# Sparse attention stage: unscaled weights turned, the three branches' values kept apart, scale factors formed later and applied to the results

## The chip, the cores and the metric

One core of a Trainium2 chip runs the whole program. The metric is the device time of one execution in microseconds (us). TensorE (PE in the rows) does matrix products and transposes, VectorE (DVE) and ScalarE (ACT) elementwise work, GpSimd (POOL) and SyncE (SP) issue the transfers (DMA) beside what else they do. The engines run on their own and meet only at semaphores.

## The reference, cut to what matters

The model is one hybrid decoder layer: a convolution branch, a gated DeltaNet branch, sparse attention, then cross attention and an MLP. The change touches sparse attention alone. Its part for the prompt, for each of 8 heads and each of 8 blocks of 128 queries, with three branches of keys (compressed, selected, window):

```python
def masked_softmax(s, mask):
    s = jnp.where(mask, s.astype(F32), -1e30)
    m = jnp.max(s, axis=-1, keepdims=True)
    e = jnp.exp(s - m) * mask
    return e / jnp.maximum(jnp.sum(e, axis=-1, keepdims=True), 1e-30)
...
o_c = jnp.einsum('bgrqn,bngd->bqgrd', p_c.astype(vc.dtype), vc)
o_s = jnp.einsum('bgrqk,bgqkd->bqgrd', p_s.astype(vs.dtype), vs)
...
gt = jax.nn.sigmoid(gl).reshape(Bh, Th, 3, NSA_KV, NSA_GQ, 1)
...
o = gt[:, :, 0] * o_c + gt[:, :, 1] * o_s + gt[:, :, 2] * o_w
```

So each branch's exponentials are divided by their row sum, multiplied by that branch's gate and by the values, and the three results are added. The division and the gate are one factor for each query, branch and head. The factor can be applied to the exponentials (before) or to the branch's result (after).

## The kernel before

The sparse stage is the function `sparse`. It works on a list of 50 items in a fixed order: 32 prompt items (4 head pairs of 8 query blocks `tt`; one item holds both key groups `g`) and 18 sets of the sample's cache pages (items of kind SET), which stand between the prompt items from the fifth on, two sets for three prompt items. A prompt item has `tt + 1` blocks of 128 selected keys, up to 5 window blocks, and 4(tt + 1) compressed keys. Everything is float32.

The same order of steps is written out by hand on three engines:

- TensorE, step i: `score(i, c)` writes the scores of item i in chunks of up to 512 columns into a ring of two bank pairs (chunk G waits until chunk G - 2 has been read: `pe.wait_ge(biased, G - 1)`). Between the chunks, `merged` puts the tail of item i - 3: `turn` transposes its weights in groups of two key blocks, `values` multiplies them with the values, two groups later. One bank region collects all three branches of an item.
- VectorE, step i: `biases(i)` adds the position bias to each chunk, takes the maxima, and ends with the negated maximum (`negm_ready`). Then `scales(i - 1)` waits until ScalarE has all exponentials of item i - 1, forms the six factors (three small instructions, L2071 to L2075), and multiplies the exponentials with them in six instructions (L2080), whereupon `probs_ready` lets TensorE turn them.
- ScalarE, step i: `exps(i - 1)` (six exponentials with their sums, L1911), interleaved with `copies(i - 3)`, the copies of the turned weights out of the PSUM banks (L1931), and `keep_result` (L1949), the copy of a finished item to the output.

The factor on the exponentials is this:

```python
last = V.tensor_scalar(src, src, scale[:, p, g, x:x + 1], None, ALU.mult)
```

SyncE's queue loads, in order of the item that frees the place, the pages of the sets (a ring of three sets of 2 MB, shared with GpSimd's queue) and, for each new head pair, queries and bias rows (`load(r)`: 5 transfers, 2.2 MB).

Of the kernel before, what the change touches and what calls it, by code (L numbers as in the profile page):

```python
# [13 lines left out]
ALU = mybir.AluOpType  # L14
# [8 lines left out]
P = 128  # L23
# [1521 lines left out]
def sparse(nc, t, u, kv, toeplitz, ident, by_token, out, gdn, spill, kvp, space, pages, kct, vc_past, past_space, early):  # L1545
# [15 lines left out]
    PAGES, NEWKEYS = "pages", "new"  # L1561
# [40 lines left out]
    first_chunk, first_group = [0], [0]  # L1602
    for i in range(NI):
        first_chunk.append(first_chunk[-1] + n_chunks(i))
        first_group.append(first_group[-1] + len(groups(i)))
    BEHIND = 2
# [7 lines left out]
    with ExitStack() as ctx:  # L1614
# [12 lines left out]
        assert next_place(nc) - ranking_at >= 3 * 16 * PAGE * 2 and early.end - early.at >= 16 * PAGE * 2  # L1627
# [5 lines left out]
        cnt, flag, addm, near = S("count", [P, IH]), S("flag", [P, NBLK]), S("block_mask", [P, 2, NBLK]), S("near", [P, 2, PAGE])  # L1633
        oc, acc = S("set_out", [P, 2, 2, P]), S("sample_sum", [P, 2, P])
# [4 lines left out]
        def alias(name, shape):  # L1639
# [5 lines left out]
        ring = alias("ring", [P, 2, HB, 4, 2 * PAGE])  # L1645
        third = nc.alloc_sbuf_tensor_at("nsa_ring_third", [P, HB - 1, 4, 2 * PAGE], F32, offset=ranking_at)
        third_last = nc.alloc_sbuf_tensor_at("nsa_ring_third_last", [P, 4, 2 * PAGE], F32, offset=early.at)
# [9 lines left out]
        region = lambda i: ps[:, O_BANK + i % REGIONS, 0:P]  # L1657
        sem = phase_semaphores(ctx, nc, "nsa_")
# [5 lines left out]
        (scores_mm, biased, cleared, max_ready, negm_ready, exp_ready, chain, probs_ready, pt_mm, pt_out, pv_mm, o_mm, o_out) = (  # L1664
            sem(s) for s in ("scores_mm", "biased", "cleared", "max_ready", "negm_ready", "exp_ready", "chain", "probs_ready",
                             "pt_mm", "pt_out", "pv_mm", "o_mm", "o_out"))
# [71 lines left out]
        def _(pe):  # L1738
# [3 lines left out]
            def score(i, c):  # L1742
                kind, n, tt = items[i]
                G = first_chunk[i] + c
# [42 lines left out]
            def values(i, k):  # L1787
# [16 lines left out]
                else:  # L1804
                    for j, (x, col, vb) in enumerate(group):
                        w = 4 * (tt + 1) if x == CMP else P
                        for g in range(2):
# [61 lines left out]
            for i in range(NI + LAG):  # L1869
# [11 lines left out]
                tailing = [(i - LAG, s) for s in range(0, len(groups(i - LAG)), 2)] if i >= LAG else []  # L1881
                for which, (n, k) in merged(scoring, tailing):
                    if which:
# [3 lines left out]
                        values_up_to(first_group[n] + pair[-1] + 1 - BEHIND)  # L1887
                    else:
# [8 lines left out]
        def _(act):  # L1897
# [43 lines left out]
            def keep_result(i):  # L1941
                kind, n, tt = items[i]
                act.wait_ge(o_mm, i + 1)
                if kind == SET:
                    x, hf, c = sets[n]
                    dst = oc_set[:, hf, c, :] if x == SLC else oc[:, hf, 0, :]
                else:
                    dst = out[:, n, tt * P:(tt + 1) * P]
                act.activation(dst, region(i), ACT.Copy).then_inc(o_out, 1)  # L1949
# [48 lines left out]
        def _(dve):  # L1998
# [13 lines left out]
            def set_biases(i):  # L2012
                x, hf, c = sets[items[i][1]]
                G, dst = first_chunk[i], s_[:, i % SLOTS, 0, :]
# [12 lines left out]
                add_biases(stat_of(items[i][1]), pieces, (biased, first_chunk[i + 1])).then_inc(negm_ready, 1)  # L2027

            def biases(i):
# [12 lines left out]
                for c, pieces in enumerate(chunks(tt)):  # L2042
                    G = first_chunk[i] + c
# [13 lines left out]
                dve.wait_ge(biased, first_chunk[i + 1])  # L2057
# [119 lines left out]
            for i in range(NI + 1):  # L2177
# [4 lines left out]
                if i >= 1:  # L2182
                    scales(i - 1)
# [1012 lines left out]
```

## Time and profile before

| | us |
|---|---|
| median of 3 runs (2793.57 to 2802.07) | 2799.81 |
| the profiled execution | 2800.31 |
| its span | 2798.6 |
| sparse stage within it, from its first matmul to ScalarE's last copy | 1060.7 to 1441.6 |
| its steady part in the rows below | 1093 to 1440 |

The profiled execution is 0.50 above the median, and 1.71 of it lie outside the span. The rows are of this one execution. Busy shares of engines within the steady part (347 us) say how full each is; the waits say which engine was late. "[2.83 <-ACT ...]" behind a row of the timeline is the idle time of that engine ahead of this instruction, and what ended it.

### The profile page before, as it was taken

To read this page: it belongs to the slowest core of one execution; us is meant where nothing else is said; L and a number is where in the kernel's file an instruction comes from. 1 tells how busy PE (TensorE), PEld (TensorE's weight loads), DVE (VectorE), ACT (ScalarE), POOL (GpSimd) and SP (SyncE) were. 2 spreads that over 40 slices of the span, in tenths; PEclk is the share of its full clock that TensorE was granted. 3 is DMA by queue.
4 is the path that set the end of the run, shared out by engine and by line. 5 is a ranking of instruction groups with operands and counts; after the bars stand their busy time and mean duration, and the time that the engine had idled before them with its cause. 6 is when DMAs were issued, how large, how long until landed. Compare 5 with 4: busy or idle time off the path is not lost. (4 is left out here: it accounts for less than half of the span.)

```text
span 2798.6 us, 52706 instructions
## 1 busy us (share of the span) xinstructions
PE 2621.9 (94%) x21842; PEld 2422.9 (87%) x21842; DVE 1318.0 (47%) x2314; ACT 853.8 (31%) x1606; POOL 701.9 (25%) x554
## 2 busy tenths in 40 slices
PE   8999999999889887898879999999999999999997
PEld 7999999999867774555559999988999999999996
DVE  6989999313134357456543453234333323224233
ACT  5323111113123334665642132144221121120222
POOL 2222222222144331212104325201522222222222
PEclk9999999999969898999989999999999999999998
DMA  5122352332287636434335441243111111111111
GB/s 187 46 69 56 105 105 87 93 92 77 95 268 228 205 105 238 150 118 148 104 112 177 137 172 54 68 166 114 46 46 46 46 46 46 46 46 46 46 46 70
DMA packets 149345, 290.33 MB, mean 104 GB/s; under 512 B 28356, under 2 KB 97160, under 8 KB 146354
## 3 DMA queue, kind: packets, MB, share of 16 engines
q1 hardware_dynamic: 137586, 255.49, 28.8%
q0 software_dynamic: 11520, 31.47, 3.6%
q8 instruction: 173, 2.83, 0.4%
q14 instruction: 66, 0.54, 0.1%
HBM read 245.94 MB, written 51.93 MB: 106 GB/s over the span
## 5 line engine op out<-in xcount | busy, mean ns | idle before, releaser
L147 POOL TENSOR_TENSOR mlp_w_low<-mlp_w_raw,mlp_w_high 128x1024 fp32r<-128x1024 f32 x72 | 173.6, 2411 | 649.4 <-ACT mlp_w_high L143 649.4
L373 PE MATMUL in_psum<-x_high,in_w_high 128*128 128x352 f32 x1416 | 265.9, 329 | 21.7 <-DVE x_low L568 11.7
L147 POOL TENSOR_TENSOR in_w_low<-in_w_raw,in_w_high 128x1024 fp32r<-128x1024 f32 x59 | 146.9, 2490 | 547.3 <-ACT in_w_high L143 547.3
L143 ACT ACTIVATE mlp_w_high<-mlp_w_raw 128x1024 fp32r<-128x1024 f32 x72 | 76.4, 1061 | 621.5 <-PE mlp_psum L2850 621.5
L2850 PE MATMUL mlp_psum<-mlp_in,mlp_w_high 128*128 128x352 f32 x1536 | 264.9, 324 | 0.0
L373 PEld LDWEIGHTS in_psum<-x_high,in_w_high 128*128 128x128 f32 x1416 | 236.5, 191 | 29.9 <-issue 15.4
L373 PE MATMUL in_psum<-x_low,in_w_high 128*128 128x352 f32 x1416 | 261.3, 326 | 0.0
L373 PE MATMUL in_psum<-x_high,in_w_low 128*128 128x352 f32 x1416 | 258.7, 324 | 0.0
L2850 PEld LDWEIGHTS mlp_psum<-mlp_in,mlp_w_high 128*128 128x128 f32 x1536 | 251.2, 189 | 0.2
L373 PEld LDWEIGHTS in_psum<-x_low,in_w_high 128*128 128x128 f32 x1416 | 237.4, 191 | 0.0
L373 PEld LDWEIGHTS in_psum<-x_high,in_w_low 128*128 128x128 f32 x1416 | 234.6, 189 | 0.0
L2618 PE MATMUL mix_psum<-branch_halves,mix_w_high 128*128 128x352 f32 x960 | 179.3, 327 | 11.9 <-DVE branch_halves L2703 8.6
L527 DVE SCALAR_TENSOR_TENSOR branches<-glu_prompt,conv_a_taps,branches 128x1024 f32<-128x1024 f32 x120 | 189.6, 1580 | 0.0
L147 POOL TENSOR_TENSOR mix_w_low<-mix_w_raw,mix_w_high 128x1024 fp32r<-128x1024 f32 (+1 forms) x56 | 109.8, 1962 | 306.1 <-ACT mix_w_high L143 306.1
L2850 PE MATMUL mlp_psum<-hidden_high,mlp_w_high 128*128 128x352 f32 x960 | 178.0, 324 | 1.8 <-PEq L86 1.8
L2850 PE MATMUL mlp_psum<-hidden_high,mlp_w_low 128*128 128x352 f32 x960 | 177.8, 324 | 0.0
L2850 PE MATMUL mlp_psum<-hidden_low,mlp_w_high 128*128 128x352 f32 x960 | 177.8, 324 | 0.0
L143 ACT ACTIVATE in_w_high<-in_w_raw 128x1024 fp32r<-128x1024 f32 x59 | 62.4, 1057 | 366.1 <-PE in_psum L373 350.2
L2618 PEld LDWEIGHTS mix_psum<-branch_halves,mix_w_high 128*128 128x128 f32 x960 | 161.0, 191 | 12.6 <-issue 12.4
L2850 PEld LDWEIGHTS mlp_psum<-hidden_high,mlp_w_high 128*128 128x128 f32 x960 | 159.0, 189 | 2.0 <-issue 2.0
L2850 PEld LDWEIGHTS mlp_psum<-hidden_high,mlp_w_low 128*128 128x128 f32 x960 | 159.2, 189 | 0.0
L2850 PEld LDWEIGHTS mlp_psum<-hidden_low,mlp_w_high 128*128 128x128 f32 x960 | 159.0, 189 | 0.0
(493 smaller groups left out, 4429.8 us busy)
## 6 DMA issues: line engine op xcount, KB each, us to landing
mlp_w_raw<-in_w_mlp SPq DMA_DIRECT2D x64, 512.0 KB, 3.6
in_w_raw<-in_w_in SPq DMA_DIRECT2D x59, 512.0 KB, 4.2
gdnp_page_ring<-in_cache_cmp POOLq DMA_DIRECT2D x128, 128.0 KB, 4.8
gdnp_page_ring<-in_cache_cmp SPq DMA_DIRECT2D x128, 128.0 KB, 4.9
u_scratch<-stage SPq DMA_DIRECT2D x28, 528.0 KB, 5.2
aux<-u_scratch SPq DMA_DIRECT2D x24, 528.0 KB, 4.0
nsa_ring<-in_cache_slc SPq DMA_DIRECT2D x90, 128.0 KB, 4.0
nsa_ring<-in_cache_slc POOLq DMA_DIRECT2D x70, 128.0 KB, 4.1
```

Of the source, the lines that this page charges most:

```text
L143: act.activation(self.high[:, i % 2, 0:k * P], self.raw[:, i % 2, 0:k * P], ACT.Copy).then_inc(self.rounded, 1)
L147: self.nc.gpsimd.tensor_tensor(self.low[:, i % 2, 0:k * P], self.raw[:, i % 2, 0:k * P], self.high[:, i % 2, 0:k * P].bitcast(F32), ALU.su ...
L373: return mm(psum[:, e % 2, n, 0:WN], w[:, i % 2, c * P:(c + 1) * P], a[:, c, n * WN:(n + 1) * WN], start=x == 0 and c == 0, stop=x == 2 an ...
L527: V.scalar_tensor_tensor(out=y, in0=src, scalar=w, in1=y, op0=ALU.mult, op1=ALU.add).then_inc(conv_chain, 1)
L2618: return mm(psum[:, e % 2, n, 0:cols.stop - cols.start], w[:, i % 2, c * P:(c + 1) * P], a(c)[:, cols], start=x == 0 and c == 0, stop=x == ...
L2850: return mm(psum[:, e % 2, n, 0:WN], w[:, i % 2, c * P:(c + 1) * P], a(c)[:, column(n)], start=x == 0 and c == 0, stop=x == 2 and c == CHU ...
```

## The change

Turned and multiplied are now the unscaled exponentials: `turn` waits for `exp_ready` instead of `probs_ready`, and the six instructions of L2080 are gone. `values` writes the three branches into three separate 128-column regions of the item's bank (`by_branch`), with as many matmuls as before. ScalarE copies all three regions (128x384 instead of 128x128) into `weighed`, a ring of two, after it has waited that the prompt item two before has been combined (`prompt_out`). VectorE forms the factors of item i - 3 in step i (`scales`), where it was item i - 1. In step i TensorE spreads the factors of item i - 5 over the 64 rows of each group by six matmuls with the identity (`factors`); they take one place of the two-pair ring of score banks, behind the score chunks of the step. VectorE then multiplies the copied results with them and adds the three branches (`combine`: one 128x384 product, one 128x384 reduction to 128x128). Two steps follow at the end for the last two items. `load(r)` now waits for the last maxima of head pair r - 2 (`negm_ready`) instead of its last result (`o_out`). The tiles `block_mask`, `near` and the sample's sum moved to other addresses.

```diff
@@ -1599,11 +1599,19 @@
+    of_step = lambda step: step - LAG - 2
+    STEPS = NI + LAG + 2
+    combined = lambda step: of_step(step) >= 0 and items[of_step(step)][0] == PROMPT
+    chunk_at, factors_at, n_all_chunks, first_group = [], {}, 0, [0]
+    for step in range(STEPS):
+        chunk_at.append(n_all_chunks)
+        n_all_chunks += n_chunks(step) if step < NI else 0
+        if combined(step):
+            factors_at[step] = n_all_chunks
+            n_all_chunks += 1
...
-    BEHIND = 2
+    BEHIND, BEFORE_SCALES = 2, 3
...
+        by_branch = lambda i: ps[:, O_BANK + i % REGIONS, 0:3 * P].rearrange("p (x n) -> p x n", x=3)
...
                 if r >= 2:
-                    sp.wait_ge(o_out, last_of_head[r - 2] + 1)
+                    sp.wait_ge(negm_ready, last_of_head[r - 2] + 1)
...
+            def factors(step):
+                G, n = factors_at[step], prompts_before[of_step(step)]
+                if G >= 2:
+                    pe.wait_ge(biased, G - 1)
+                pe.wait_ge(scale_ready, n + 1)
+                for x in range(3):
+                    for g in range(2):
+                        last = mm(score_bank(G, 0)[g * DH:(g + 1) * DH, x * P:(x + 1) * P],
+                                  scale[:, n % SLOTS, g, x:x + 1].to_broadcast([P, DH]), ident[:, :], start=True, stop=True)
+                last.then_inc(scores_mm, 1)
...
                 if k == 0:
-                    pe.wait_ge(*((probs_ready, prompts_before[i + 1]) if kind == PROMPT else (exp_ready, i + 1)))
+                    pe.wait_ge(exp_ready, i + 1)
...
-                            last = mm(region(i)[dims, :], v, pt[0:w, G % TSLOTS, 2 * j + g, :], start=k == 0 and j == 0, stop=x == CMP)
+                            last = mm(by_branch(i)[dims, x, :], v, pt[0:w, G % TSLOTS, 2 * j + g, :], start=vb == first_block,
+                                      stop=x == CMP or vb == tt)
...
                 scoring = [(i, c) for c in range(n_chunks(i))] if i < NI else []
-                tailing = [(i - LAG, s) for s in range(0, len(groups(i - LAG)), 2)] if i >= LAG else []
+                if i in factors_at:
+                    scoring.append((i, FACTORS))
+                tailing = [(i - LAG, s) for s in range(0, len(groups(i - LAG)), 2)] if LAG <= i < NI + LAG else []
+                if i == NI + LAG:
+                    values_up_to(first_group[NI])
...
-            values_up_to(first_group[NI])
             for hf in range(2):
                 pe.wait_ge(sum_ready, hf + 1)
-                pe.wait_ge(biased, first_chunk[NI])
+                pe.wait_ge(biased, n_all_chunks)
...
-                    dst = out[:, n, tt * P:(tt + 1) * P]
-                act.activation(dst, region(i), ACT.Copy).then_inc(o_out, 1)
+                before = prompts_before[i]
+                if before >= 2:
+                    act.wait_ge(prompt_out, before - 1)
+                act.activation(weighed[:, before % 2, :, :], by_branch(i), ACT.Copy).then_inc(o_out, 1)
...
-                dve.wait_ge(chain, 3 * n + 4)
-                for g in range(2):
-                    for x, at, w in spans(tt):
-                        src = s_[:, i % SLOTS, g, at:at + w]
-                        last = V.tensor_scalar(src, src, scale[:, p, g, x:x + 1], None, ALU.mult)
-                last.then_inc(probs_ready, 1)
+            def combine(step):
+                m = of_step(step)
+                kind, r, tt = items[m]
+                G, n = factors_at[step], prompts_before[m]
+                dve.wait_ge(scores_mm, G + 1)
+                dve.wait_ge(o_out, m + 1)
+                rows = weighed[:, n % 2, :, :]
+                V.tensor_tensor(rows, rows, score_bank(G, 0)[:, 0:3 * P].rearrange("p (x n) -> p x n", x=3), ALU.mult).then_inc(biased, 1)
+                dve.wait_ge(biased, G + 1)
+                V.tensor_reduce(out[:, r, tt * P:(tt + 1) * P], rows.rearrange("p x n -> p n x"), AX_X, ALU.add
+                                ).then_inc(prompt_out, 1)
...
-            for i in range(NI + 1):
+            for i in range(STEPS):
...
-                if i >= 1:
-                    scales(i - 1)
+                if BEFORE_SCALES <= i < NI + BEFORE_SCALES:
+                    scales(i - BEFORE_SCALES)
+                if i in factors_at:
+                    combine(i)
```

What this does to VectorE's order, at one place: the stretch holds the end of `biases` of a prompt item (tt = 4), the scaling of the prompt item before it (tt = 3), and the first instruction of a set's biases (L2007 before, L2041 after). Before:

```order
L2061 TENSOR_SCALAR nsa_negmax<-nsa_max 128x6
L2071 TENSOR_SCALAR nsa_scale<-nsa_sums 128x6
L2073 RECIPROCAL nsa_scale<-nsa_scale 128x6
L2075 TENSOR_TENSOR nsa_scale<-nsa_scale,by_token 128x6
L2080 TENSOR_SCALAR nsa_probs<-nsa_probs,nsa_scale 128x512 x2
L2080 TENSOR_SCALAR nsa_probs<-nsa_probs,nsa_scale 128x16
L2080 TENSOR_SCALAR nsa_probs<-nsa_probs,nsa_scale 128x512 x2
L2080 TENSOR_SCALAR nsa_probs<-nsa_probs,nsa_scale 128x16
L2007 ISA nsa_probs,nsa_set_part_max<-nsa_psum,nsa_block_mask 128x512
```

The same place on VectorE after the change:

```order
L2095 TENSOR_SCALAR nsa_negmax<-nsa_max 128x6
L2105 TENSOR_SCALAR nsa_scale<-nsa_sums 128x6
L2107 RECIPROCAL nsa_scale<-nsa_scale 128x6
L2109 TENSOR_TENSOR nsa_scale<-nsa_scale,by_token 128x6
L2118 TENSOR_TENSOR nsa_weighed<-nsa_weighed,nsa_psum 128x384
L2120 TENSOR_REDUCE branches<-nsa_weighed 128x128
L2041 ISA nsa_probs,nsa_set_part_max<-nsa_psum,nsa_block_mask 128x512
```

The six products on the exponentials of the item one before have become two instructions on the result of the item five before; the small three now belong to the item three before.

On TensorE, the steps around the first set's score (L1752 before, L1766 after). Before:

```order
L1784 MATMUL nsa_psum<-ident,nsa_probs 128x128 x8
L1810 MATMUL nsa_psum<-nsa_probs_t,nsa_v_by_token 64x128 x2
L1810 MATMUL nsa_psum<-nsa_probs_t,nsa_v_cmp 64x128 x2
L1752 MATMUL nsa_psum<-nsa_ring,early_q_padded 32x512 x4
L1784 MATMUL nsa_psum<-ident,nsa_probs 8x128 x2
L1810 MATMUL nsa_psum<-nsa_probs_t,nsa_v_by_token 64x128 x8
```

After, where L1809 is the transposes, L1836 the values and L1788 the new factors:

```order
L1766 MATMUL nsa_psum<-nsa_ring,early_q_padded 32x512 x4
L1809 MATMUL nsa_psum<-ident,nsa_probs 128x128 x8
L1836 MATMUL nsa_psum<-nsa_probs_t,nsa_v_by_token 64x128 x2
L1836 MATMUL nsa_psum<-nsa_probs_t,nsa_v_cmp 64x128 x2
L1788 MATMUL nsa_psum<-ident,nsa_scale 64x128 x6
L1809 MATMUL nsa_psum<-ident,nsa_probs 8x128 x2
L1836 MATMUL nsa_psum<-nsa_probs_t,nsa_v_by_token 64x128 x8
```

The set's score moved ahead of a group of transposes, since the factors count as one more scoring piece of the step, and six matmuls stand later in the same step.

## Rows read from the trace of the kernel before

**Rows 1.** Windows: busy us and count by engine, granted clock (PEclk), DMA share, GB/s

```profile
1093.00:1440.00 347.00, 303.39 (x3062) 196.82 (x3059) 205.07 (x959) 221.45 (x637) 57.34 (x105) 0.93 0.36 114
```

**Rows 2.** Waits from 1093 to 1440: total us, times, longest us

```profile
ACT nsa_probs L1911 <- DVE nsa_negmax L2061: 54.1, 24, 6.4
...
DVE nsa_scale L2071 <- ACT nsa_probs L1911: 34.3, 20, 3.5
...
PE nsa_psum L1763 <- DVE nsa_part_max L2054: 23.7, 18, 3.7
...
PE nsa_psum L1784 <- ACT nsa_probs_t L1931: 6.9, 14, 1.1
PE nsa_psum L1752 <- DMA nsa_ring_third<-in_cache_slc: 6.6, 1, 6.6
PE nsa_psum L1784 <- DVE nsa_probs L2080: 5.5, 7, 2.0
```

**Rows 3.** Timeline at 1133 and 1300: start us, us, instruction, idle before

```profile
1133.09 0.61 PE L1763 MATMUL nsa_psum<-early_k_cmp,nsa_q_heads 64*128 64x16 f32 x4 [2.48 <-DVE nsa_part_max L2054]
...
1133.63 1.97 PE L1784 MATMUL nsa_psum<-ident,nsa_probs 128*128 128x128 f32 x8
...
1300.36 0.17 DVE L2071 TENSOR_SCALAR nsa_scale<-nsa_sums 128x6 f32<-128x6 f32 x1 [2.83 <-ACT nsa_probs L1911]
...
1301.00 2.23 DVE L2080 TENSOR_SCALAR nsa_probs<-nsa_probs,nsa_scale 128x640 f32<-128x640 f32 x6
...
1303.13 0.68 DVE L2054 CUSTOM_DVE_ANT_0 nsa_probs<-nsa_psum,nsa_bias_full 128x512 f32<-128x512 f32 x1
...
1304.49 0.92 PE L1763 MATMUL nsa_psum<-nsa_k_prompt,nsa_q_heads 64*128 64x384 f32 x4 [1.99 <-DVE nsa_part_max L2054]
```

**Rows 4.** Window of 10 us around the first of these places, columns as before

```profile
1130.00:1140.00 10.00, 7.52 (x60) 4.65 (x55) 4.82 (x21) 3.78 (x12) 1.07 (x2) 0.61 0.06 17
```

**Rows 5.** SyncE's queue from 1170, and its wait ahead of the first row

```profile
1170.33 0.33 SPq L1711 DMA_DIRECT2D nsa_q_heads<-u_scratch  x1
...
1176.53 1.39 SPq L1702 DMA_DIRECT2D nsa_ring_third<-in_cache_slc  x3
...
SPq L1711 <- ACT branches L1949: 11.9, 1, 11.9
```

**Rows 6.** Instructions of L2080 from 1056 to 1446: busy us and count

```profile
1056.00:1446.00 390.00, 64.11 (x192) 0.92 0.41 135
```

**Rows 7.** Groups by shape from 1060 to 1446: busy us, mean ns

```profile
L2054 DVE CUSTOM_DVE_ANT_0 nsa_probs<-nsa_psum,nsa_bias_full 128x384 f32<-128x384 f32 x16 | 8.3, 553 | 3.8 <-PE nsa_psum L1763 3.8
...
L2080 DVE TENSOR_SCALAR nsa_probs<-nsa_probs,nsa_scale 128x1024 f32<-128x1024 f32 x8 | 6.0, 750 | 0.1
...
L1931 ACT ACTIVATE nsa_probs_t<-nsa_psum 128x512 f32<-128x512 f32 x146 | 86.0, 591 | 59.4 <-PE nsa_psum L1784 38.6 <-PE nsa_psum L1777 9.8 <-PE nsa_psum L1810 7.6
...
L1949 ACT ACTIVATE branches<-nsa_psum 128x128 f32<-128x128 f32 x32 | 8.4, 264 | 1.1 <-PE nsa_psum L1810 0.9
```

**Rows 8.** Timeline of the stage's start: VectorE and TensorE

```profile
1080.52 0.16 DVE L2071 TENSOR_SCALAR nsa_scale<-nsa_sums 128x6 f32<-128x6 f32 x1
...
1082.19 0.28 DVE L2146 TENSOR_REDUCE nsa_score<-nsa_psum 128x64 f32<-128x128 f32 x1
...
1089.53 3.78 PE L1763 MATMUL nsa_psum<-nsa_k_prompt,nsa_q_heads 64*128 64x512 f32 x12 [8.70 <-DVE nsa_part_max L2054]
```

**Rows 9.** Timeline of the stage's end: TensorE and ScalarE

```profile
1435.27 1.09 PE L1784 MATMUL nsa_psum<-ident,nsa_probs 128*128 128x128 f32 x8
...
1436.29 1.09 PE L1810 MATMUL nsa_psum<-nsa_probs_t,nsa_v_by_token 128*64 128x128 f32 x16
...
1437.31 0.79 PE L1784 MATMUL nsa_psum<-ident,nsa_probs 128*128 128x128 f32 x4
...
1439.63 0.44 PE L1894 MATMUL nsa_psum<-ident,nsa_sample_sum 128*128 128x128 f32 x2
...
1439.75 0.28 ACT L1949 ACTIVATE branches<-nsa_psum 128x128 f32<-128x128 f32 x1 [0.59 <-PE nsa_psum L1810]
```

More of the change, by code:

```diff
@@ L1560, in sparse @@
     PROMPT, SET = range(2)
-    PAGES, NEWKEYS = "pages", "new"
+    PAGES, NEWKEYS, FACTORS = "pages", "new", "factors"
     sets = [(x, hf, c) for hf in range(2) for x, c in [(WIN, 0)] + [(SLC, c) for c in range(NCH)]]
@@ L1626, in sparse @@
         lower, gtm, eqm = (sb(ctx, nc, "nsa_" + n, [P, IH, NBLK], dt) for n, dt in (("lower", U16), ("greater", BF16), ("equal", BF16)))
-        assert next_place(nc) - ranking_at >= 3 * 16 * PAGE * 2 and early.end - early.at >= 16 * PAGE * 2
+        assert next_place(nc) - ranking_at >= 3 * 16 * PAGE * 2 + 8 * NBLK and early.end - early.at >= 16 * PAGE * 2
         gates24, gates = S("gates24", [P, 2, 3, NSA_HEADS]), S("gates", [P, 2, 3])
@@ L1632, in sparse @@
         inv, score, scol = S("inv", [P, 2]), S("score", [P, NBLK]), S("score_col", [P, IH])
-        cnt, flag, addm, near = S("count", [P, IH]), S("flag", [P, NBLK]), S("block_mask", [P, 2, NBLK]), S("near", [P, 2, PAGE])
-        oc, acc = S("set_out", [P, 2, 2, P]), S("sample_sum", [P, 2, P])
+        cnt, flag = S("count", [P, IH]), S("flag", [P, NBLK])
+        oc, weighed = S("set_out", [P, 2, 2, P]), S("weighed", [P, 2, 3, P])
+        assert NCMP == P
+        acc = sc
         least, weight, total, coef = S("least", [P, 2]), S("weight", [P, 2, NCH]), S("total", [P, 2, NCH + 4]), S("coef", [P, 2, NCH + 2])
@@ L1645, in sparse @@
         ring = alias("ring", [P, 2, HB, 4, 2 * PAGE])
+        near = alias("near", [P, 2, PAGE])
+        assert place[0] <= space + 2 * 4 * 4 * W
         third = nc.alloc_sbuf_tensor_at("nsa_ring_third", [P, HB - 1, 4, 2 * PAGE], F32, offset=ranking_at)
+        addm = nc.alloc_sbuf_tensor_at("nsa_block_mask", [P, 2, NBLK], F32, offset=ranking_at + 3 * 16 * PAGE * 2)
         third_last = nc.alloc_sbuf_tensor_at("nsa_ring_third_last", [P, 4, 2 * PAGE], F32, offset=early.at)
@@ L1663, in sparse @@
             "k_in", "v_turned", "v_ready", "vc_turned", "vc_ready", "spilled"))
-        (scores_mm, biased, cleared, max_ready, negm_ready, exp_ready, chain, probs_ready, pt_mm, pt_out, pv_mm, o_mm, o_out) = (
-            sem(s) for s in ("scores_mm", "biased", "cleared", "max_ready", "negm_ready", "exp_ready", "chain", "probs_ready",
-                             "pt_mm", "pt_out", "pv_mm", "o_mm", "o_out"))
+        (scores_mm, biased, cleared, max_ready, negm_ready, exp_ready, chain, scale_ready, pt_mm, pt_out, pv_mm, o_mm, o_out, prompt_out) = (
+            sem(s) for s in ("scores_mm", "biased", "cleared", "max_ready", "negm_ready", "exp_ready", "chain", "scale_ready",
+                             "pt_mm", "pt_out", "pv_mm", "o_mm", "o_out", "prompt_out"))
         (lower_in, zeroed, bias_mm, bias_ready, m0_mm, m0_read, turned_mm, turned, past_mm,
@@ L1868, in _ @@
             pe.wait_ge(k_in, 32)
-            for i in range(NI + LAG):
+            for i in range(STEPS):
                 if i == LAG:
@@ L1887, in _ @@
                         values_up_to(first_group[n] + pair[-1] + 1 - BEHIND)
+                    elif k == FACTORS:
+                        factors(n)
                     else:
                         score(n, k)
-            values_up_to(first_group[NI])
             for hf in range(2):
                 pe.wait_ge(sum_ready, hf + 1)
-                pe.wait_ge(biased, first_chunk[NI])
+                pe.wait_ge(biased, n_all_chunks)
                 tr(ps[:, hf, 0:P], acc[:, hf, :], ident[:, :]).then_inc(final_mm, 1)
@@ L2026, in set_biases @@
                         pieces += [(dst[:, at:BANK], src[:, at:BANK], near[:, hf, :]), new(1)]
-                add_biases(stat_of(items[i][1]), pieces, (biased, first_chunk[i + 1])).then_inc(negm_ready, 1)
+                add_biases(stat_of(items[i][1]), pieces, (biased, chunk_at[i] + 1)).then_inc(negm_ready, 1)
             def biases(i):
@@ L2163, in masks @@
                 dve.wait_ge(spread_mm, 1)
+                dve.wait_ge(spilled, 16)
                 for hf in range(2):
@@ L2176, in _ @@
             dve.wait_ge(chain, 1)
-            for i in range(NI + 1):
+            for i in range(STEPS):
                 if i == RANKED:
```

21 lines of the change are left out of this document (10 added, 11 removed).

## Prediction, made before the run

> **What bounds the kernel now.** I looked first at the stretch that the edited functions fill: the sparse stage, 1060.7 to 1441.6 us. The rest of the span, before and behind it, runs the same instructions in both kernels, so all of the difference has to arise here. In its steady part no engine is full: TensorE is busy 303.4 of 347 us, VectorE 205.1, ScalarE 221.5, and TensorE's granted clock is 0.93 [rows 1]. TensorE has the longest day, so the time that counts is its idle time, 347 - 303.4 = 43.6 us, plus the time its work is stretched by the lower clock.
>
> The table of waits splits the idle time [rows 2]. 23.7 us go to scores (L1763) that wait until VectorE has read an older chunk; 5.5 us to transposes that wait for VectorE's scaled weights; 6.9 us to transposes that wait for ScalarE's copies; 6.6 us, in one piece, to pages that had not landed. These are 42.7 of the 43.6.
>
> Why VectorE is late shows in two more rows of that table: it waits 34.3 us for ScalarE's exponentials, while ScalarE waits 54.1 us for VectorE's maxima. They wait on each other in turn. The timeline shows one such place [rows 3]: at 1300.36 VectorE has lost 2.83 us waiting for the exponentials of the last item, then needs until 1303.13 to form factors and scale; only then does it touch the next item's scores. TensorE's next chunk comes at 1304.49 after 1.99 us of idling. The first rows show the same with 2.48 us, and what follows it: 8 transposes take 1.97 us, where at full clock they take 1.09 [rows 9]. The window around it has a granted clock of 0.61 [rows 3, 4]: part of it at 1.2 GHz, part at 2.4 GHz, after TensorE had stood still.
>
> **The change, part by part.** All sums are made against the profiled execution, 2800.3 us; the median of the runs is 0.5 lower.
>
> *VectorE's load.* The 192 scalings go, 64.1 us [rows 6]. Each of 32 prompt items gets a 128x384 product and a 128x384 reduction. Neither stands in the trace; the nearest row, 384 columns out of PSUM with a second operand, takes 553 ns [rows 7], so 32 x 2 x 0.553 = 35.4 us. Net, VectorE loses 29 us of work. It is not on the path itself; what counts is the waits that it causes.
>
> Per element the new work is dearer: 553/384 = 1.44 ns against 750/1024 = 0.73 ns for the scaling of the largest piece [rows 7]. The Trainium skill (VectorE: DVE Perf Modes, The perf-mode tier table) says why and speaks against the change: a float32 scaling from SBUF runs in the double mode, a two-tensor product and a reduction only in the single one. The rows agree; at equal rates one would have expected a saving larger than 29 us by about half of the 35.
>
> *The exponentials' wait.* In step i VectorE now asks for item i - 3, which ScalarE finished two steps ago, where it asked for item i - 1. So the 34.3 us of waiting leave VectorE's stream, and with them the order in which VectorE must finish scaling before it reads the next scores. Behind those instructions stood the next item's biases, and behind these ScalarE's exponentials and TensorE's scores. At the place at 1300 VectorE would start 2.83 + 2.77 us earlier, and TensorE's 1.99 us vanish. The 5.5 us of waits for scaled weights can't exist any more: -5.5. Of the 23.7 us I take away 17 and leave 7: where a light tail (a set) stands beside four score chunks, VectorE's own rate per chunk stays the limit, and `combine` (1.1 us) stands ahead of the next biases. Bounds: 0 and -23.7.
>
> *New matmuls.* Per prompt item six, each 128 columns by 64 rows of output, in pairs for the two groups, as the values (L1810). The rows of the trace count two per float32 matmul; 16 such rows take 1436.29 to 1437.31 = 1.02 us at full clock, transposes following at once [rows 9]. 12 rows take 12/16 of it, 0.77 us, and 32 items 24.5 us. It lies on TensorE, the busiest engine: +24.5. Bounds: nothing, if all falls into waits that remain (7 + 6.9 us can hide at most 14), and 49 at half the clock.
>
> *ScalarE's copy.* 128x384 for 128x128: between 264 and 591 ns [rows 7], by columns 482, so +0.22 x 32 = 7 us on an engine that is busy 64%. Hidden behind its 54.1 us of waiting for maxima, in most places. With the new wait for `prompt_out` in front of it, ahead of the next copies of turned weights, for which TensorE waits, I take +3 in all (the 6.9 us of such waits grow by under half). Bounds: 0 and +7.
>
> *SyncE's queue.* The wait of the third head pair's load for `o_out` cost 11.9 us, and the load's 2.2 MB then went out at 1170.33, right ahead of the pages for the ring's third place, which SyncE issued at 1176.53 [rows 5]. It is these pages that TensorE waited 6.6 us for [rows 2]. With `negm_ready` the wait is over before SyncE reaches it, the load goes into the idle stretch before 1170, and the pages follow as soon as their place is free. I take -6; bounds 0 and -6.6. Issues stay the same in number and order; GpSimd's queue is not touched.
>
> *Start.* The scaling of item 0 (1080.52 to 1082.19) stands ahead of the ranking and of the biases for which TensorE waits 8.70 us [rows 8]: -1.7. The scaling of item 1 stands right behind them; -1.3 more, since TensorE still has scores of its own then. Together -3.
>
> *Clock.* 0.07 x 347 = 24 us of clock are missing in the steady part [rows 1], times TensorE's busy share of 0.87 about 21 us of stretch. The low stretches follow TensorE's longer stops. If the stops go at a good third of the places, -8. Bounds 0 and -21.
>
> *End.* Before, ScalarE copies the last item at 1439.75, 0.28 us, and goes on to the sample's rows, already turned at 1439.63 [rows 9]. After, two rounds of factors (1.54 us) follow the last values, `combine` of the second last item (1.1), the last product (0.55), and only then the two final transposes (0.44), which need the banks: the first round is out at 1440.4, so 1442.5 instead of 1440.0: +2.5.
>
> Sum: 24.5 - 5.5 - 17 + 3 - 6 - 3 - 8 + 2.5 = -9.5, which gives 2790.8, and 2790 against the median.
>
> **Rivals.**
> *The ring of score banks (slower).* `factors` takes one of two bank pairs in 32 of 55 steps and holds it until VectorE has done biases, maxima, factors and the product. If TensorE's waits on VectorE stay at 23.7 us, only under this new name, and the clock stays too, the sum is 24.5 - 5.5 + 3 - 6 - 3 + 2.5 = +15.5: 2815. For it: TensorE waits already on this ring, and gets 32 entries beside the 106 score chunks that the list of items makes. Against it: VectorE's stream is 29 us lighter and no longer stops for ScalarE. It decides from about 16 us of such waits on; below, the kernel isn't slower.
> *The waits move to ScalarE (same).* ScalarE runs exponentials and copies in one line; once VectorE is on time they come in a heap, and TensorE's transposes wait. If 9 of the 17 us come back so: 2799. For it: TensorE waits 6.9 us so already, in 14 places [rows 2], and ScalarE gets 7 us more work. Against it: it is 64% busy on the whole [rows 1].
> *The clock stays up (much faster).* If the short stops that remain no longer pull the clock down, the clock term is -21 instead of -8 and with less left of the waits for VectorE (3 us instead of 7) the sum is -26.5; half way there, -18: 2782. For it: with VectorE's long stops and the page wait gone, few stops of over 2 us are left.
> The Trainium skill (TensorE: Matmul & The Clock Gate, What's actually happening) has it that activity releases the throttle and that idling brings it back. The rows agree in kind: 0.61 around a stop, 0.93 on the mean.
> *The load changes nothing*: the pages could be late for their own 2 MB. Then 6 us of the sum stay away, 2796; it is within the forecast's own range.
>
> **How the numbers follow.** 0.3% is 8.4 us, about what a measurement of this kernel can tell from no change, so faster means below 2791.4 and slower above 2808.2. Forecast 0.45, own range 2783 to 2798, a bit more than half of it faster (0.26). Clock stays up 0.25, all faster. Waits to ScalarE 0.18, same. Ring 0.12, slower. Faster 0.51, same 0.37, slower 0.12. The range leaves out the ring's far end and the far end of the fast case: 2772 to 2804.
>
> **What would show it.** In the profile after: VectorE busy near 176 in the steady part; no wait of VectorE's factors on ScalarE, and none of transposes on VectorE; waits of scores on VectorE under 10 us; no wait for pages near 1183, and the third head pair's load ahead of 1165; a granted clock of 0.95 or more; the new matmuls at 0.77 us a round; ScalarE's copy near 480 ns. The stage would end near 1432. It would be wrong if the new rounds wait long for VectorE (the ring), or if the transposes' waits for copies double.

## The result, and the profile after

The changed kernel takes 2767.98 us (median of 4 runs, 2764.02 to 2768.74); the kernel before took 2797.99 us beside it (2793.57 to 2802.07). The ratio is 0.9894, 95% interval 0.9883 to 0.9906: 30.0 us less. The prediction said 9.5 us less and its range ended at 2772, so the direction was right and the size was not. The profiled execution took 2767.28 us. Its page begins:

```profile
span 2765.6 us, 53441 instructions
...
PE 2623.4 (95%) x22226; PEld 2432.9 (88%) x22226; DVE 1292.0 (47%) x2186; ACT 859.8 (31%) x1606; POOL 701.6 (25%) x554
```

To compare kernels I use one stretch, cut at the same two instructions in each: from the row of 12 scores that follows the first long stop [rows 8] to the start of the last copies of the sample. It always holds the same 3070 TensorE instructions of each kind, plus 384 where the factors' matmuls are in. The first row is the kernel before, the second the changed one; columns as in [rows 1].

```profile
1089.53:1440.00 350.47, 306.86 (x3070) 198.77 (x3070) 208.39 (x972) 222.05 (x639) 57.34 (x105) 0.93 0.36 116
```

```profile
1088.60:1408.62 320.02, 308.42 (x3454) 209.39 (x3454) 182.43 (x853) 228.09 (x639) 56.31 (x105) 0.99 0.39 126
```

The stretch is 30.45 us shorter, which is nearly the whole result. TensorE's idle time went from 350.47 - 306.86 = 43.6 us to 320.02 - 308.42 = 11.6 us. The odd thing is its busy time: 384 more matmul instructions, and only 1.6 us more. The granted clock explains it: 0.93 before, 0.99 after. VectorE is busy 26 us less, ScalarE 6 us more.

The mean hides how the clock is spread. Cut at the places where it changes, the stretch before holds nine pieces at 0.50, the lower level (1.2 GHz); two of them and the sum of all nine:

```profile
1132.20:1142.30 10.10, 9.21 (x62) 6.31 (x64) 3.93 (x19) 4.08 (x11) 2.92 (x6) 0.50 0.27 84
1186.90:1193.60 6.70, 4.58 (x26) 2.45 (x28) 0.85 (x3) 1.31 (x4) 0.00 (x0) 0.50 0.51 158
...
sum 48.47, PE 44.10 PEld 25.55 DVE 22.54 ACT 19.20 POOL 2.92; mean PE 4.90 PEld 2.84 DVE 2.50 ACT 2.13 POOL 0.32
```

The changed kernel has one, behind the stop at the start, and then the upper level to the end:

```profile
1088.60:1092.75 4.15, 4.15 (x14) 2.43 (x15) 2.03 (x10) 0.60 (x2) 0.00 (x0) 0.50 1.10 348
1092.80:1408.62 315.82, 304.22 (x3441) 206.91 (x3440) 180.35 (x844) 227.49 (x637) 56.31 (x105) 1.00 0.38 123
```

So TensorE was busy for 44.1 us at the lower level before, and is for 4.2 us now. Work at that level takes about twice its time (12 rows of scores 3.78 us [rows 8], and 1.99 us at 1275.39 in the changed kernel), so the low clock cost about 22 us before and costs about 2 us now: an estimate of 20 us won. The new matmuls then take 1.6 + 20, about 21.6 us of TensorE's busy time.

The waits of the changed kernel from 1090 to 1408 (total us, times, longest us):

```profile
DVE nsa_probs L2088 <- PE nsa_psum L1777: 75.1, 48, 3.5
...
DVE nsa_weighed L2118 <- PE nsa_psum L1788: 24.4, 16, 8.5
...
ACT nsa_probs L1943 <- DVE nsa_negmax L2095: 15.6, 16, 2.7
...
PE nsa_psum L1809 <- ACT nsa_probs_t L1963: 5.6, 10, 1.4
PE nsa_psum L1777 <- DVE nsa_part_max L2088: 1.9, 3, 0.7
PE nsa_psum L1788 <- DVE nsa_part_max L2088: 1.6, 4, 0.4
PE nsa_psum L1905 <- ACT nsa_weighed L1983: 0.7, 1, 0.7
```

Set against [rows 2]: scores waited 23.7 us for VectorE, now 1.9, and the factors 1.6. The waits for scaled weights (5.5) and for pages (6.6) are gone. VectorE no longer waits for exponentials (34.3) but for scores, 75.1 us: it now stands ready ahead of TensorE. ScalarE's wait for maxima fell from 54.1 to 15.6. TensorE has at last become the engine that the others wait for.

The timeline shows how a step now looks; before, VectorE stood idle for 2.83 us until the exponentials of this same item were there, and then scaled for over 2 us [rows 3]:

```profile
1268.71 0.82 PE L1788 MATMUL nsa_psum<-ident,nsa_scale 128*64 128x128 f32 x12
...
1269.07 0.17 DVE L2095 TENSOR_SCALAR nsa_negmax<-nsa_max 128x6 f32<-128x6 f32 x1
1269.15 0.17 DVE L2105 TENSOR_SCALAR nsa_scale<-nsa_sums 128x6 f32<-128x6 f32 x1
1269.27 0.83 ACT L1943 ACTIVATE nsa_probs<-nsa_probs,nsa_negmax 128x640 f32<-128x640 f32 x1 [0.35 <-DVE nsa_negmax L2095]
...
1269.66 0.55 DVE L2118 TENSOR_TENSOR nsa_weighed<-nsa_weighed,nsa_psum 128x384 f32<-128x384 f32 x1
...
1270.24 0.59 DVE L2120 TENSOR_REDUCE branches<-nsa_weighed 128x128 f32<-128x384 f32 x1
```

After the maxima at 1269.07 VectorE goes straight into the factors of an older item (1269.15), their product with another item's results and the sum, without an idle time in any bracket, while ScalarE makes the new item's exponentials at 1269.27.

The prices of the new work, groups by shape (busy us, mean ns | idle before):

```profile
L1788 PE MATMUL nsa_psum<-ident,nsa_scale 128*64 128x128 f32 x384 | 27.0, 276 | 1.7 <-DVE nsa_part_max L2088 1.6
...
L2120 DVE TENSOR_REDUCE branches<-nsa_weighed 128x128 f32<-128x384 f32 x32 | 19.0, 594 | 1.1
L2118 DVE TENSOR_TENSOR nsa_weighed<-nsa_weighed,nsa_psum 128x384 f32<-128x384 f32 x32 | 17.7, 552 | 24.7 <-PE nsa_psum L1788 24.4
...
L1983 ACT ACTIVATE nsa_weighed<-nsa_psum 128x384 f32<-128x384 f32 x32 | 15.3, 477 | 1.1 <-PE nsa_psum L1836 1.0
```

SyncE's queue, and then the start and the end of the stage:

```profile
1153.87 0.43 SPq L1725 DMA_DIRECT2D nsa_q_heads<-u_scratch  x1
...
1168.68 1.39 SPq L1716 DMA_DIRECT2D nsa_ring_third<-in_cache_slc  x3
```

```profile
1088.60 3.79 PE L1777 MATMUL nsa_psum<-nsa_k_prompt,nsa_q_heads 64*128 64x512 f32 x12 [7.00 <-DVE nsa_part_max L2088]
...
1405.21 0.43 PE L1836 MATMUL nsa_psum<-nsa_probs_t,nsa_v_cmp 32*64 32x128 f32 x4
1405.57 1.53 PE L1788 MATMUL nsa_psum<-ident,nsa_scale 128*64 128x128 f32 x24
...
1408.28 0.46 PE L1926 MATMUL nsa_psum<-ident,nsa_past_scores 128*128 128x128 f32 x2 [1.18 <-DVE nsa_weighed L2118]
```

The third head pair's load left 16.5 us earlier than in [rows 5] and the pages behind it 7.9 us earlier (2.3 us of both is the stage's earlier start in this execution). The first stop shrank from 8.70 [rows 8] to 7.00 us. At the end, the last values are followed by both rounds of factors (1.53 us) and a stop of 1.18 us, as the prediction drew it.

### The profile page after: what moved, and what is told of

Same layout as the page of the kernel before. It is cut to its first block and busy times, and to the rows that moved or that the text cites. A ratio compares the mean times of both kernels' runs of the same rounds, so it can differ in the third digit from the quotient of the medians.

```text
span 2765.6 us, 53441 instructions
## 1 busy us (share of the span) xinstructions
PE 2623.4 (95%) x22226; PEld 2432.9 (88%) x22226; DVE 1292.0 (47%) x2186; ACT 859.8 (31%) x1606; POOL 701.6 (25%) x554
## 5 line engine op out<-in xcount | busy, mean ns | idle before, releaser
L373 PE MATMUL in_psum<-x_high,in_w_high 128*128 128x352 f32 x1416 | 266.1, 330 | 21.4 <-DVE x_low L568 11.4
L2661 PEld LDWEIGHTS mix_psum<-branch_halves,mix_w_high 128*128 128x128 f32 x960 | 160.5, 191 | 12.4 <-issue 12.2
```

Of the source, the lines that this page charges most:

```text
L373: return mm(psum[:, e % 2, n, 0:WN], w[:, i % 2, c * P:(c + 1) * P], a[:, c, n * WN:(n + 1) * WN], start=x == 0 and c == 0, stop=x == 2 an ...
L2661: return mm(psum[:, e % 2, n, 0:cols.stop - cols.start], w[:, i % 2, c * P:(c + 1) * P], a(c)[:, cols], start=x == 0 and c == 0, stop=x == ...
```

## The experiments

The theories. *A:* two things made TensorE stop: VectorE's load, and its wait for exponentials ahead of the next biases; and the stops lower the clock, which costs more on top. Rivals: *the load alone*, *the order alone*, and *the matmuls' price* (the new matmuls cost little since TensorE had room). Each number named "stretch" is cut as above; times are medians, and differences to the changed kernel are to its 2767.98, to the one before to the runs beside.

**The load line alone, and undone.** Two kernels: before with the new line, the changed kernel with the old one.

```diff
-                    sp.wait_ge(o_out, last_of_head[r - 2] + 1)
+                    sp.wait_ge(negm_ready, last_of_head[r - 2] + 1)
```

> The kernel before with the new condition of the head pair's load alone. Theory 'queue': the 6.6 us wait for pages goes, with the low clock behind it 7 to 9 us less than 2798. Rival (the pages were late for their own 2 MB): 0 to -1 us.

> The changed kernel with the old condition of the head pair's load (its last result). Theory 'queue': a wait for pages of 5 to 8 us comes back near 1170 and the time rises by 5 to 8 us, to 2773 to 2776. Rival (the stage's new pace hides it): 2768.

The first took 2795.94 us (10 runs), ratio 0.9985 (0.9968 to 1.0002); the second 2780.7 us, 12.7 more than the changed kernel. Their stretches:

```profile
1096.22:1441.25 345.03, 307.79 (x3070) 200.59 (x3070) 208.51 (x972) 221.66 (x639) 57.30 (x105) 0.93 0.36 115
```

```profile
1091.57:1419.83 328.26, 310.04 (x3454) 209.94 (x3454) 182.44 (x853) 228.23 (x639) 56.32 (x105) 0.98 0.38 121
```

and of its waits:

```profile
PE nsa_psum L1766 <- DMA nsa_ring_third<-in_cache_slc: 6.6, 1, 6.6
```

On the kernel before, the line takes 5.4 us from the stretch; the medians differ by 2.4 us, less than the 7 to 9 expected, and the interval of the ratio just holds no change. In the changed kernel the same stop of 6.6 us comes back, and 8.2 us of stretch with it. Of the profiled executions' 12.6 us the other 4.4 lie 3.0 ahead of the stretch and 1.4 behind it, where both kernels run the same; I count them to neither. The wait itself goes and comes as drawn, so the step of the prediction holds, at -5 to -8 of stretch. The clock falls behind this stop too (the row from 1186.90 above), but one stop costs little of it: with the stop back in the changed kernel, busy time rose by 1.6 us. Taking it out of the kernel before didn't lower busy time at all (307.8 for 306.9 us).

**The order alone.** Before, with the scaling of an item moved one step back, and then with the load line too.

```diff
-            for i in range(NI + 1):
+            for i in range(NI + 2):
...
-                if i >= 1:
-                    scales(i - 1)
+                if i >= 2:
+                    scales(i - 2)
...
```

> The kernel before, with one edit: VectorE scales item i - 2 in step i instead of item i - 1; the 192 scalings stay where they are applied, no factor matmuls. Theory 'order' (VectorE is late because it stops for ScalarE's exponentials ahead of the next biases, and TensorE's stops pull its clock down): 2770 to 2780 us against 2798, TensorE's waits on VectorE under 10 us in the steady part, granted clock there 0.97 or more. Theory 'load' (VectorE is late because it has 29 us too much work): within 5 us of 2798, waits and clock as before.

> The same edit, and the third and fourth head pair's load waits for the last maxima instead of the last result. Theory 'order' plus the page wait: 5 to 8 us below the run with the first edit alone, no wait for pages near 1183. If both hold, it stands at 2765 to 2772 without a single new matmul, level with the changed kernel or a little below. Theory 'load': 2790.

Measured: 2869.47 us, ratio 1.0254 (1.0232 to 1.0275), and 2863.68 us, ratio 1.0235 (1.0216 to 1.0254). Both theories are far off: these kernels are slower by 71 and 65 us. The stretch of the first and its largest wait of TensorE:

```profile
1092.20:1512.67 420.47, 341.52 (x3070) 223.66 (x3070) 210.83 (x981) 227.88 (x638) 56.60 (x105) 0.83 0.30 94
```

and of its waits:

```profile
PE nsa_psum L1784 <- DVE nsa_probs L2080: 76.5, 28, 5.1
```

The waits of scores on VectorE did fall, but the transposes need the scaled weights of an item that VectorE now finishes a step later: 76.5 us of waits where there were 5.5 [rows 2]. As long as the scaling stands between exponentials and transposes, and TensorE turns item i - 3, it can't be put off (a tail of item i - 4, with larger rings, was not tried). Otherwise it has to be applied to the results first, and that is what the matmuls of factors pay for. The same 3070 instructions are also busy 34.7 us longer (341.52 for 306.86), at a clock of 0.83.

**The load of VectorE alone.** Before, with only 16 columns per item and group scaled, by one instruction where there were three; the rest of the weights stay unscaled. The order is the old one, and no engine gets new work.

```diff
-                    for x, at, w in spans(tt):
-                        src = s_[:, i % SLOTS, g, at:at + w]
+                    for x, at, w in spans(tt)[-1:]:
+                        src = s_[:, i % SLOTS, g, at:at + min(w, 16)]
```

> The kernel before, with its order of VectorE's steps (exponentials' wait, factors, then the next biases) but nearly without the scaling: of the five pieces per prompt item and group only 16 columns of the last are scaled, so that about 60 of the 64.1 us of scaling leave VectorE and nothing is added to any engine; the other columns of the weights go unscaled. Theory A (VectorE's load and its wait cost together): the wait for exponentials stays (over 30 us), the waits for scaled weights go, TensorE's waits for VectorE fall from 24 to about 10 us, the clock rises to about 0.97, and the time is 2770 to 2783. Theory B (the load alone is what mattered): the whole stop goes, 2755 to 2768, and the clock is 0.99 or more. Theory C (the wait alone mattered): above 2788, with more than 18 us of TensorE's waits for VectorE left.

It took 2774.84 us, ratio 0.9918 (0.9902 to 0.9935): 22 us less than before, as theory A has it, and between the ranges of its two rivals.

```profile
1092.14:1416.61 324.47, 295.68 (x3070) 193.19 (x3070) 158.63 (x848) 221.01 (x639) 56.32 (x105) 0.96 0.38 123
```

and of its waits:

```profile
PE nsa_psum L1763 <- DVE nsa_part_max L2054: 17.5, 10, 7.9
PE nsa_psum L1784 <- ACT nsa_probs_t L1931: 11.4, 20, 1.4
```

VectorE works 50 us less, and still waits 47.8 us for exponentials. TensorE's waits on it fall from 32.4 us, with the 8.70 at the start, to 17.5 with 7.9 at the start. The waits for ScalarE's copies rise from 6.9 to 11.4: the rival "waits move to ScalarE" is real here, at half its price. Busy time falls by 11.2 us with the same instructions, so here 14.8 us fewer idle brought 11.2 us of clock.

**The distance of the factors.** The changed kernel with factors one item, and then two items, behind the scores in place of three. (At one item the factors have a ring of 8 places, and in one step the sum stands ahead of them, as the banks would otherwise wait in a circle.)

```diff
-    BEHIND, BEFORE_SCALES = 2, 3
+    BEHIND, BEFORE_SCALES = 2, 1
```

> The changed kernel with the factors formed one item behind again (scales of item i - 1 in step i, in a ring of 8; in one step `combine` stands ahead of it). VectorE's load is the light one, the wait for the exponentials is back. Theory 'order': 10 to 22 us back up, 2778 to 2790, clock near 0.95. Theory 'load': within 4 us of 2768.

> The changed kernel with the factors two items behind the scores in place of three; the work of every engine is the same. Theory A (VectorE's wait for exponentials is what gives the stops back): most of the wait of a_lag1 (53 us) is gone at two items already, since ScalarE has a whole step for the exponentials; the time lies within 4 us of the changed kernel, 2764 to 2773. Rival (every item of distance counts alike): about half way to a_lag1, 2776 to 2780, with 15 us or more of waits of VectorE's factors for exponentials.

At one item: 2786.88 us, 18.9 more than at three. At two: 2771.53 us (2764.33 to 2773.31), 3.6 more, inside what the runs scatter. First the stretch and waits at one item, then the stretch at two:

```profile
1088.39:1428.69 340.30, 318.14 (x3454) 215.00 (x3454) 183.92 (x850) 228.17 (x638) 56.49 (x105) 0.97 0.37 120
```

and of its waits:

```profile
DVE nsa_scale L2107 <- ACT nsa_probs L1944: 53.0, 25, 5.2
...
PE nsa_psum L1778 <- DVE nsa_part_max L2089: 6.5, 7, 3.8
PE nsa_psum L1789 <- DVE nsa_part_max L2089: 5.9, 8, 2.6
```

```profile
1089.74:1409.85 320.11, 308.18 (x3454) 208.99 (x3454) 182.22 (x853) 228.26 (x639) 56.50 (x105) 1.00 0.39 124
```

With one item VectorE's wait for exponentials is back, 53.0 us. The work of every engine is that of the changed kernel, and yet the stretch is 20.3 us longer: 10.6 us more idle, and 9.7 us more busy with the same 3454 instructions. This is the cleanest evidence for the order, and for the clock. At two items the stretch is as long as at three, within 0.1 us, and no wait of the factors for exponentials is left: it falls away at once, not by degrees. One item of slack is enough here, and the third buys nothing that these runs can tell.

**VectorE loaded again.** The changed kernel with three useless reductions behind each prompt item's factors.

```diff
+                for k, cols in enumerate((768, 768, 256)):
+                    V.tensor_reduce(spare[:, k:k + 1], bias[:, 0:cols], AX_X, ALU.max)
```

> The changed kernel with three useless reductions behind the factors of each prompt item (768, 768 and 256 columns of a constant tile, about 2.2 us, 32 times some 70 us): VectorE carries more than the scalings' 64 us again, but waits for nobody. Theory 'load': 15 us or more back up, 2783 or above. Theory 'order': part of it only, since VectorE now waits 100 us for TensorE in the steady part; 2768 to 2778.

2785.53 us, 17.5 more. The expectation of 2778 or less for "the order alone" is missed; that rival falls.

```profile
1089.01:1423.65 334.64, 312.94 (x3454) 211.38 (x3454) 246.12 (x949) 228.55 (x639) 56.50 (x105) 0.98 0.38 123
```

64 us of added work lengthen the stretch by 14.6 us, 10.1 idle and 4.5 busy, though VectorE is busy only 74% of it. So load and order both count, and they don't add up: less load with the old order gave 22 us, the new order lost 19 when taken back, and the whole is 30.

**The matmuls' price.** The changed kernel with one of three pairs of factors (those of two branches are left out, and their old numbers used); and the kernel before with 144 useless transposing matmul instructions, twelve ahead of the third score chunk of 12 items, where TensorE had stood still.

```diff
-                for x in range(3):
+                for x in range(1):
```

```diff
+                if c == 2 and i and items[i - 1][0] == SET:
...
+                    for j in range(12):
+                        tr(turn_bank(free)[:, j % 4 * P:(j % 4 + 1) * P], ident[:, :], ident[:, :])
```

> The changed kernel with one of three pairs of factor matmuls; the factors of the selected and window branches are left out (stale numbers are multiplied in their place). Measures the price of the new matmuls: two thirds of 24.5 us lie on TensorE. If TensorE is the bound now, 14 to 17 us less, 2751 to 2754. If the matmuls fill waits, less than 6 us.

> The kernel before with 12 useless transposes of the identity into the free turning bank ahead of the third score chunk of each of the 12 prompt items that follow a set: work for TensorE in the place of its longest stops (1.3 us at full clock each, 15 us in all). Theory 'clock' (the stops pull the clock down): granted clock in the steady part up from 0.93 to 0.96 or more and the time at or below 2798 although 15 us of work were added. If the stops have nothing to do with the clock, it stays at 0.93 and the time is 2798 to 2805.

The first took 2761.19 us, 6.8 less than the changed kernel, between the two expectations; the second 2795.94 us (10 runs), ratio 1.0003 (0.9987 to 1.0018).

```profile
1093.37:1404.83 311.46, 296.07 (x3198) 195.81 (x3198) 181.57 (x853) 227.11 (x638) 56.32 (x105) 0.99 0.40 127
```

```profile
1087.55:1435.02 347.47, 318.48 (x3214) 212.15 (x3214) 208.53 (x972) 221.46 (x638) 57.33 (x105) 0.95 0.37 118
```

Two thirds of the factors' instructions are gone, but a round of 4 rows takes more than a third of a round of 12: their group falls from 27.0 to 13.0 us, and TensorE's busy time by 12.4 us (308.42 to 296.07). The stretch is 8.6 us shorter and holds 3.8 us more idle time: about two thirds of the price shows. On the kernel before, added matmuls cost nothing: they filled stops (43.6 us idle became 29.0), and the clock rose from 0.93 to 0.95, not quite to the 0.96 expected. "+24.5 us on the busiest engine" was therefore an upper price.

**Two tries for more.** First the final transposes into banks that are free, so that they need not wait for the last product; then, on top of it, the ranking's two comparisons moved behind the biases of steps 2 and 3.

```diff
-                pe.wait_ge(biased, n_all_chunks)
-                tr(ps[:, hf, 0:P], acc[:, hf, :], ident[:, :]).then_inc(final_mm, 1)
+                tr(ps[:, 4 + hf, 0:P], acc[:, hf, :], ident[:, :]).then_inc(final_mm, 1)
```

```diff
+                if i == 2:
+                    V.tensor_tensor(gtm[:, :, :], row, col, ALU.is_gt)
                 if i == 3:
+                    ranked(V.tensor_tensor(eqm[:, :, :], row, col, ALU.is_equal))
+                if i == 4:
                     count()
```

> The changed kernel with the sample's two final transposes in the free turning banks, so that they need not wait for the last product. In the changed kernel TensorE waited 1.18 us for it and ScalarE's last copies began 3.4 us after the last values. Expected: 1 to 1.5 us less at the stage's end, too little for the timing: 2766 to 2768, a ratio to the kernel before of 0.989 as for the changed kernel.

> The same, and the ranking's two long comparisons (2.4 us each) and its count put one behind the biases of steps 2, 3 and 4 instead of both ahead of the biases of step 2. The 7.0 us for which TensorE waits there in the changed kernel should shrink to about 2 us. Theory 'order' (TensorE is the bound and every stop of it counts once, more with the clock): 3 to 6 us less, 2761 to 2765. Rival (the comparisons only move the stop to the next steps): 2766.

2767.54 and 2767.33 us: neither differs from the changed kernel by what can be measured, as expected of the first; of the second 3 to 6 us were expected, and its rival was right. In the first the end is 1.2 us shorter, as drawn (the last copies start 2.19 us after the last values, not 3.41). In the second the first stop fell from 7.00 to 2.27 us, and a new one came where the ranking's result is needed:

```profile
1088.55 3.78 PE L1777 MATMUL nsa_psum<-nsa_k_prompt,nsa_q_heads 64*128 64x512 f32 x12 [2.27 <-DVE nsa_part_max L2087]
...
PE nsa_psum L1905 <- ACT nsa_weighed L1982: 3.8, 1, 3.8
```

No kernel that computes the whole result beat the changed one by a measurable amount.

## Why the prediction was right in kind and wrong in size

The profiled executions differ by 33.0 us of span, and the sum was -9.5. Term by term, from the stretch and the waits:

```
term                          predicted   measured
scaled weights' wait            -5.5        -5.5
scores' wait for VectorE       -17         -20.2   (23.7 to 1.9 + 1.6)
new matmuls                    +24.5       +21.6   (busy +1.6, plus 20.0)
wait for ScalarE's copies       +3          -1.3   (6.9 to 5.6)
SyncE's queue, pages            -6          -6.6
start                           -3          -1.7   (8.70 to 7.00)
end                             +2.5        +1.4   (1.2, and a stop of the ranking 0.5 to 0.7)
clock                           -8         -20.0   (half of 44.1 less 4.2 us at the lower level)
```

The measured terms sum to -32.3; what is left to 33.0 lies outside the stage or in stops too small to list. The split of matmuls and clock rests on the estimate of the section on the result; their sum of 1.6 us is measured. The group of L1788 is 27.0 us long by itself, but its rows overlap their neighbours: the round at 1268.71 lasts 0.82 us and the next instruction starts at 1269.46, 0.75 us later, which makes 24.0 us for 32 rounds.

**The step that failed is the clock's.** The prediction put "about 21 us of stretch" as the most, and "If the stops go at a good third of the places, -8". The bound was good: the low clock cost about 22 us. The share was not, and the prediction named no row for a third. The stops went at all of the places: in the timeline of the stretch the kernel before has eight stops of TensorE between 1.3 and 3.8 us beside the two long ones, and the changed kernel, beside the one at the start, has two, both under 1.4. Behind seven of the eight, and behind both long ones, the clock was at its lower level; in the changed kernel only behind the one at the start. So 20 us came back and not 8, which is 12 of the 23 us by which the sum was short. The next largest parts are ScalarE's copies (4.3) and the scores' wait (3.2).

The rival "the clock stays up" had the mechanism that decided, and both of its numbers: -21 for the clock, and 3 us left of the waits for VectorE (3.5 measured). Its full sum of -26.5 was nearest, and was given 0.25 as a half-way case at 2782.

**VectorE's waits:** right in kind. The reason given, the 34.3 us of waiting for exponentials, is shown by the kernel with factors one item behind. But "a light tail beside four score chunks stays the limit" was too careful: of 7 us that should remain, 3.5 did. The load of VectorE, costed as "not on the path itself", counts on its own, as the kernels with less scaling and with the useless reductions show.

**ScalarE** was wrong in sign. It gets 6.0 us more work and TensorE waits less for its copies. No single row explains it: its wait for maxima and TensorE's waits for copies are 54.1 and 6.9 us before, 43.1 and 11.4 nearly without scaling, 15.6 and 5.6 in the changed kernel. A steadier order would fit, but that is only argued.

**The prices** were good: the product 552 ns for 553, ScalarE's copy 477 for 482, the reduction 594 for 553 (so that VectorE is busy 181 us from 1090 to 1408 where 176 were expected), a round of factors 0.75 us from its start to the next instruction for 0.77. That the new matmuls would lie wholly on the time was not: of 12.4 us of busy time taken out with two thirds of them, 3.8 came back as idle time. The sum also counts some matmuls too often: the two last rounds (1.54 us) are among the 32 of the +24.5, but the first stands in the end's +2.5 once more, and the second lies there beside VectorE's work and not on the path.

**The queue** came out as drawn: the load left ahead of 1165, and no page was waited for. The **ring of score banks** fell: factors waited 1.6 us for a bank, of the 16 from which it would have decided. **Start and end** were small, and right to 1.3 us.

What stays open is which stops bring the clock down. No run changed the clock by itself, but what it costs can be read. Idle time and busy time of the same 3454 instructions are 11.6 and 308.4 us (changed), 18.2 and 310.0 (old load line), 21.7 and 312.9 (reductions), 22.2 and 318.1 (one item). The last two have the same idle time and 5.2 us between them in busy time. The clock accounts for it: TensorE is busy at the lower level for 12.6 us with the reductions and 22.4 us at one item. Half of that, less the 2.1 of the changed kernel, is 4.2 and 9.1 us, against 4.5 and 9.7 us of added busy time. Their stops differ in kind, 3.8 and 2.6 us on VectorE against 1.8 and shorter beside one of 3.5 on ScalarE, but which trait of a stop counts, these runs don't settle; length alone it is not, since before a stop of 1.39 us was followed by 5.92 us of work at the lower level and one of 1.98 us by none. Nor did a run test the tiles that moved to other addresses. The Trainium skill (TensorE: Matmul & The Clock Gate, A second HAM failure mode: psum-queue depth-cycling) tells of a kernel whose frequent small stops between groups of matmuls made the clock swing between its two levels. The traces here agree: pieces at 0.50 between stretches at 1.00 with the stops, 1.00 without them but for the first 4 us.

## What to carry to other kernels

When TensorE's granted clock is below 1 in a stage where it idles in many short stops, cost an edit that removes them at more than the idle time: here the clock added 0.4 to 0.9 us for each us of idle time (the change 20 on 32.0, one item 9.7 on 10.6, less scaling 11.2 on 14.8, the reductions 4.5 on 10.1), and about 2 us for a single stop of 6.6. As the bound of the clock's part take half of TensorE's busy time in the pieces at the lower level, and ask of each piece whether the stop ahead of it will stay. An instruction in a strict queue that waits for another engine should stand one whole step behind what it waits for, and one step is enough; if its result is needed sooner, as the scaled weights were, first move the operation to where it is needed late. Work added to TensorE is not paid in full: here nothing showed of what was put into the stops of a stage with 12% idle time, and two thirds where 4% was idle.

## What the hardware showed that I had not expected

The same 3070 matmul instructions were busy 295.7, 306.9 and 341.5 us in three kernels, with 28.8, 43.6 and 79.0 us of idle time and a granted clock of 0.96, 0.93 and 0.83. A short stop can cost as much clock as a long one. Behind the stop of 6.6 us TensorE was busy for 4.58 us at the lower level. Behind seven of the eight stops of 1.3 to 3.8 us it was busy so for 3.3 to 9.2 us each, and without them the mean clock was back at 0.99.
